# Two stacked transformer blocks on one core: norms of the second half by tile, modulation as column factors behind the transposes, the residual's affine rows inside the stages

## The reference, cut to what matters

```python
def _modulate(x, shift, scale):
    return x * (1.0 + scale) + shift

def _post_norm(x, y, gate, res_w, gain, bias):
    return _layer_norm(ALPHA * x + res_w * (1.0 + gate) * y, gain, bias)

cond = jax.nn.silu(c)                     # c: (1, 1024)
for l in range(2):
    mod = cond @ w_ada[l] + b_ada[l]      # 9 rows of 1024: shift, scale, gate of each stage
    y = _swiglu(_modulate(x, sh1, sc1), w_gate1, w_up1, w_down1)
    x = _post_norm(x, y, g1, 0.5, ln_gain[l, 0], ln_bias[l, 0])
    y = _token_mixer(_modulate(x, sh2, sc2), w_in, w_out)
    x = _post_norm(x, y, g2, 1.0, ln_gain[l, 1], ln_bias[l, 1])
    y = _swiglu(_modulate(x, sh3, sc3), w_gate2, w_up2, w_down2)
    x = _post_norm(x, y, g3, 0.5, ln_gain[l, 2], ln_bias[l, 2])
```

## Time and profile before

| | |
|---|---|
| median of 3 runs | 2457.99 us (2457.63 to 2458.3) |
| the profiled execution | 2454.0 us, its span 2452.1 us, 1.9 us around it |
| PE busy | 2270.1 us (93%), mean granted clock 0.942 |
| DVE busy | 1641.0 us (67%) |
| ACT busy | 1147.1 us (47%) |
| POOL busy | 23.9 us (1%) |
| chain that ended last | PE 86%, DVE 10%, ACT 2%, issue 1%, DMA 1% |

### The profile page before, as it was taken

One profiled execution on the slowest core, in us unless ns is written; L12 is line 12 of the kernel. 1 busy time (PEld: TensorE's weight loads), 2 busy tenths in 40 slices (PEclk: granted clock), 3 DMA queues, 4 the chain that ended last, 5 costly groups with the idle time before them and its releaser, 6 DMA issues.

```text
span 2452.1 us, 35119 instructions
## 1 busy us (share of the span) xinstructions
PE 2270.1 (93%) x13340; PEld 2022.6 (82%) x13340; DVE 1641.0 (67%) x1804; ACT 1147.1 (47%) x1433; POOL 23.9 (1%) x14
## 2 busy tenths in 40 slices
PE   7999997999999999879999998978998998968997
PEld 6889996788888899868888888967887887967886
DVE  6775766677677576657766776547776666555666
ACT  5545442545554553345544543534444554443553
POOL 0000000000000000000000000000000000000000
PEclk9998997999999999879998998979999999978999
DMA  7774320476577532108746773404763545512543
GB/s 307 287 272 142 105 102 1 189 288 246 206 290 283 184 111 103 35 25 318 282 155 253 286 272 129 172 17 182 297 249 127 199 179 188 173 52 86 199 177 120
DMA packets 59091, 446.63 MB, mean 182 GB/s; under 512 B 6912, under 2 KB 7296, under 8 KB 8320
## 3 DMA queue, kind: packets, MB, share of 16 engines
q1 hardware_dynamic: 59008, 445.45, 48.7%
HBM read 444.38 MB, written 1.05 MB: 182 GB/s over the span
## 4 chain that ended last, share of the span: by engine, by line
PE 86%; DVE 10%; ACT 2%; issue 1%; DMA 1%; POOL 0%; POOLq 0%; DVEq 0%; SPq 0%; ACTq 0%
PE ps L225 25%; PE ps L298 14%; PE ps L230 13%; PE ps L304 7%; PE ps L260 3%; PE ps L266 3%; PE ps L261 3%; PE ps L1638 2%; PE ps L280 2%; PE ps L506 2%; PE ps L207 1%; PE ps L208 1%; PE ps L213 1%; PE ps L690 1%; DVE arena L1247 1%
## 5 line engine op out<-in xcount | busy, mean ns | idle before, releaser
L192 DVE TENSOR_TENSOR w_lo<-raw,w_hi 128x1024 fp32r<-128x1024 f32 x670 | 804.9, 1222 | 395.6 <-ACT w_hi L186 395.5
L186 ACT ACTIVATE w_hi<-raw 128x1024 fp32r<-128x1024 f32 x670 | 694.4, 1052 | 496.5 <-PE ps L304 150.8
L225 PE MATMUL ps<-hT,w_hi 128*128 128x512 f32 x2752 | 687.3, 392 | 0.5 <-ACT w_hi L186 0.5
L225 PEld LDWEIGHTS ps<-hT,w_hi 128*128 128x128 f32 x2752 | 499.4, 189 | 93.3 <-ACT w_hi L186 1.0
L230 PEld LDWEIGHTS ps<-hT,w_lo 128*128 128x128 f32 x2752 | 375.4, 190 | 26.8
L230 PE MATMUL ps<-hT,w_lo 128*128 128x256 f32 x2752 | 383.7, 282 | 0.0
L298 PE MATMUL ps<-w_hi,act_hi 128*128 128x512 f32 x640 | 198.5, 391 | 0.0
L298 PE MATMUL ps<-w_hi,act_lo 128*128 128x512 f32 x640 | 197.6, 390 | 0.0
L304 PE MATMUL ps<-w_lo,act_hi 128*128 128x512 f32 x640 | 171.0, 389 | 0.0
L260 PE MATMUL ps<-w_hi,hT 128*128 128x256 f32 (+1 forms) x576 | 146.8, 290 | 2.6 <-issue 2.6
L261 PE MATMUL ps<-w_hi,hT 128*128 128x256 f32 (+1 forms) x576 | 145.1, 288 | 0.0
(11 more groups left out here) (315 smaller groups left out, 2689.4 us busy)
## 6 DMA issues: line engine op xcount, KB each, us to landing
raw<-in_g SPq DMA_DIRECT2D x88, 1024.0 KB, 4.9
raw<-in_u SPq DMA_DIRECT2D x88, 1024.0 KB, 4.9
raw<-in_d SPq DMA_DIRECT2D x88, 1024.0 KB, 6.9
arena<-in_w_ada SPq DMA_DIRECT2D x48, 1536.0 KB, 7.6
raw<-in_w_in SPq DMA_DIRECT2D x54, 1024.0 KB, 4.9
raw<-in_w_out SPq DMA_DIRECT2D x16, 1024.0 KB, 4.9
rows<-in_rows SPq DMA_DIRECT2D x13, 1024.0 KB, 9.6
arena<-in_con SPq DMA_DIRECT2D x1, 1344.0 KB, 5.5
```

Of the source, the lines that this page charges most:

```text
L186: nc.scalar.activation(w_hi[:, buf, 0:width], raw[:, slot, half * UNIT:half * UNIT + width], ACT.Copy).then_inc(unit_hi, 1)
L192: nc.vector.tensor_tensor(w_lo[:, buf, 0:width], raw[:, slot, half * UNIT:half * UNIT + width], w_hi[:, buf, 0:width].bitcast(F32), ALU.su ...
L225: nc.tensor.matmul(o, h_[:, k, c], hT[:, :, 4 * half + k, :], start=(half == k == 0), stop=False)
```

## The change

Between the stages of the second block:
- `ln_dve` goes tile by tile: gate product for tile 0 as soon as `acc_half` comes, then ALPHA * x added with the sum over columns as `accum_out`, minus the mean as a [128, 1] column; ACT squares with that column as bias and sums, then the root; DVE writes x = (tok - mean) / std. Gain and bias are not applied there.
- PE transposes `x` itself (`pre2_pe`), and `pre2_dve` applies gain * (1 + scale) and bias * (1 + scale) + shift as per-partition column factors (`gb`) when it copies the transposed blocks from PSUM to `tok`, 16 operations of 128 columns per boundary; the hi and lo split then reads `tok`.
- The residual's gain and bias rows (`affine`, two operations of 1024 columns per tile) go into the next stage: rounds 9 and 10 of an FFN, column blocks 4 to 7 of a mixer. After the last stage they follow the norm, and the output leaves in two DMAs.
- Only the gate is spread into a row, by 8 matmuls (`gate_pe`) into banks 6 and 7, copied by `gate_act` after the splits.

The modulation product is laid out transposed: `cond` is a row on all partitions, and a chunk is three multiplications of 1024 columns whose `accum_out` is one column each of `modc`, so `ada`, `cols_pe` and `cols_dve` go, in the first block too. POOL adds the bias and makes `gb` (`cols_pool`). Apart from that: `home` numbers the unit buffers through all stages, so that the next stage's unit 0 is split (`first_hi`, `first_lo`) ahead of the norm; `x` is loaded in two DMAs, `cond` later; the second block's constants are loaded in stage 6 and no longer ahead of it.

```diff
+    def first_hi(a, B, loads):
+        hi_unit(a, B, 0, 0, loads[0] + 1, 0)
+    def first_lo(v, B):
+        lo_unit(v, B, 0, 0, 0)
...
-    def pre2_dve(v, g, B):
-        shift, scale1 = mrow[:, 0, :], mrow[:, 1, :]
-        v.wait_ge(x_ready, g * 16 + 16)
-        v.wait_ge(mod_a.sem, mod_a.at("rows", g - 6))
-        nc.vector.tensor_tensor(tok[:], x[:], over(scale1, [P, TILES, D], 1), ALU.mult).then_inc(pre2_v.done("scaled"), 1)
-        v.wait_ge(pre2_v.sem, pre2_v.at("scaled", g - 6))
-        for tile in range(TILES):
-            nc.vector.tensor_tensor(tok[:, tile, :], tok[:, tile, :], shift, ALU.add).then_inc(
-                pre_v.done(f"tok{tile}"), 1)
-        pre_lo(v, g, B)
+    def pre2_pe(pe, g):
+        for name, tile, b in PIECES:
+            if b.start == 0:
+                pe.wait_ge(x_ready, g * 16 + 8 * tile + 8)
+            for k in range(4 * b.start, 4 * b.stop):
+                last = nc.tensor.transpose(tile_bank(tile)[:, k // 4, k % 4, :], x[:, tile, k * P:(k + 1) * P], IDENT)
+            last.then_inc(pre_t.done(f"trans{name}"), 1)
...
+    def pre2_dve(v, g):
+        h = g - 6
+        v.wait_ge(mod_p.sem, mod_p.at("shift", h))
+        for name, tile, b in PIECES:
+            v.wait_ge(pre_t.sem, pre_t.at(f"trans{name}", g))
+            for k in range(4 * b.start, 4 * b.stop):
+                last = nc.vector.tensor_scalar(tok[:, tile, k * P:(k + 1) * P], tile_bank(tile)[:, k // 4, k % 4, :],
+                                               gb[:, h, 0, k:k + 1], gb[:, h, 1, k:k + 1], ALU.mult, ALU.add)
+            last.then_inc(pre2_v.done(f"t{name}"), 1)
...
     def ln_act(a, h):
...
+            nc.scalar.activation(hidden[:].rearrange("p a b -> p (a b)"), tok[:, tile, :], ACT.Square,
+                                 bias=stat[:, tile:tile + 1], accum_out=stat[:, 2 + tile:3 + tile]).then_inc(
+                                     ln_a.done(f"ssq{tile}"), 1)
...
+    def ln_dve(v, h, ready):
+        v.wait_ge(gate_a, h + 1)
...
+            if tile == 0:
+                v.wait_ge(acc_half, h + 7)
+            else:
+                v.wait_ge(*ready)
...
+            nc.vector.scalar_tensor_tensor(tok[:, tile, :], x[:, tile, :], ALPHA, tok[:, tile, :], ALU.mult, ALU.add,
+                                           accum_out=stat[:, tile:tile + 1]).then_inc(ln_v.done(f"mixed{tile}"), 1)
...
+            nc.vector.tensor_scalar(x[:, tile, :], tok[:, tile, :], stat[:, tile:tile + 1], stat[:, 2 + tile:3 + tile],
+                                    ALU.add, ALU.mult).then_inc(x_ready, 8)
...
     def chunk_dve(v, n, k):
...
-            nc.vector.scalar_tensor_tensor(ada, ada_w, cond[:, bass.ds(k, 1)], ada, ALU.mult,
-                                           ALU.add).then_inc(ada_acc, 1)
...
+        for b in range(3):
+            block = ada_w[:, b * D:(b + 1) * D]
+            last = nc.vector.scalar_tensor_tensor(
+                block, block, 1.0, cond[:], ALU.mult, ALU.mult,
+                accum_out=modc[:, n, b:b + 1] if k is first_chunk else modc[:, n, bass.ds(k * 3 + b, 1)])
+        last.then_inc(ada_acc, 1)
...
+    def gate_act(a, h, half):
+        a.wait_ge(gate_t, h + 1)
```

More of the change, by code:

```diff
@@ L162, in build @@
     post_v = steps("post_v", "gained0 rstd0 gained1 rstd1")
[L163 to L167 removed]
+    pre2_v = steps("pre2_v", "t0 t1a t1b")
+    ln_v = steps("ln_v", "gated0 mixed0 neg0 gated1 mixed1 neg1 rstd0 rstd1")
+    ln_a = steps("ln_a", "table ssq0 root0 ssq1 root1")
+    gate_t, gate_a = sem("gate_t"), sem("gate_a")
+    resid = steps("resid", "gained0 added0 gained1 added1")
+    out_v = steps("out_v", "gained0 added0 gained1 added1")
+    mod_p = steps("mod_p", "biased scale gain bias shift")
     def settle(eng):
@@ new lines, in affine, with resid_dve @@
+    def affine(v, S, use, tile, which):
+        if which == 0:
+            nc.vector.tensor_tensor(x[:, tile, :], x[:, tile, :], rows[:, 0, :], ALU.mult).then_inc(S.done(f"gained{tile}"), 1)
+        else:
+            v.wait_ge(S.sem, S.at(f"gained{tile}", use))
+            nc.vector.tensor_tensor(x[:, tile, :], x[:, tile, :], rows[:, 1, :], ALU.add).then_inc(S.done(f"added{tile}"), 1)
+    def resid_dve(v, g, tile, which):
+        if tile == which == 0:
+            v.wait_ge(rows_in, g * 16 + 16)
+        affine(v, resid, g - 7, tile, which)
```

477 lines of the change are left out of this document (246 added, 231 removed).

## The result

The changed kernel runs in **2391.82 us** (median of 4 runs, 2388.78 to 2392.5) against 2458.14 (4 runs, 2457.63 to 2459.61) for the kernel before: ratio **0.9726**, 95% interval 0.9714 to 0.9738. The forecast was 2395 with a range of 2383 to 2420. The profiled execution of the changed kernel took 2392.5 us, its span is 2390.7 where it was 2452.1, and the granted clock 0.943 where it was 0.942.

A forecast was written before the change was run, and what follows sets the result against it. PE was taken as the bound, busy 93%, with its boundary waits set by a DVE chain. Gains of 61.7 + 3 + 4 + 2 less 8 for the clock make 62.7, so 2458.0 - 62.7 = 2395 us, range 2383 to 2420.

The forecast's parts named there:

- The boundary's chain: Second block's six boundaries, timed from tile 0's last matmul (T = 0): a shorter DVE chain gains 61.7 us.
- The term of the clock: Second block's six entries: PE's half clock low 4 us each in the weights, taking 8 us back, ends 0 and 16.
- The end: After the last stage: norm, affine operations and half the output end at T = 17.0 instead of 20.0, gain 3 us.
- First block and start: Column matmuls gone ahead of transposes at three boundaries, gain 4 us; ACT's first table load gone at the start, gain 2.
- Costs put at nothing: Work moved inside the stages on DVE, ACT and POOL, and the early split of unit 0: cost 0.
- Chunks: FFN rounds, 48 times: 4.4 us of DVE work for 3.4, within 3.2 us spare, cost 0; 48 us without cover.
- Affine rows inside the stages: Residual rows add 2.4 us per FFN round, in rounds without a modulation chunk, less than the chunk they replace; cost 0.
- Rival (a): DVE's accumulating form is slow and bounds six FFN stages; at half rate, 2.57 us each, the kernel takes 2463; chance 5%.
- (c): FFN rounds: DVE's slack is not one piece, chunks delay low splits PE needs, 19 us in all, 2414; chance 8%.
- (d): Second block's entries: the clock costs nothing new, 8 us less, 2387; chance 17%.
- (b): Second block's entries: the clock's low stretch reaches further, 8 us each, costing 20 instead of 8, 2407; chance 17%.
- (e): Boundaries: chain not shortened, DVE waits for ACT's roots and factor operations take their full 0.40 us, 2408; chance 3%.

The follow-up runs named there:

- both_tiles: The changed kernel with the layer norm waiting for both tiles before its first gate product: 2407.02 us, 15.2 more than the changed kernel.
- affine_at_boundary: The changed kernel with the affine rows applied at the boundary again, not inside the stages: 2416.13 us, 24.3 more than the changed kernel.
- keep_busy: The changed kernel with unread matmuls filling PE's idle time before and after the transposes at the second block's six boundaries: 2380.61 us.
- after_again: The changed kernel run and profiled once more, nothing altered: 2392.61 us.
- split_early: The changed kernel with DVE making the low splits of pieces 0 and 1a before factors and split of 1b: 2386.76 us.
- busy_early: The changed kernel with the edits of keep_busy and split_early together: 2385.38 us.
- all_gate_later: busy_early plus filler matmuls at first-block boundaries and in both blocks' mixers, with ACT's gate row copy moved behind unit 1's high part: 2359.89 us.
- chunk_plus2: The changed kernel with two more unread DVE operations of 1024 columns in each of the 48 modulation chunks: 2397.43 us.

## Why the prediction was right, step by step

The mechanism was right, and the closeness of the number is in part luck. By profiles, 62.7 us were forecast and 61.5 came. Chain and clock brought 4.3 more than forecast, the end 1.1 more, first block and start 1.6 more; against that stand 8.2 us more in the rests of stages 0 to 5, which the sum had at nothing. Either side alone would have put it 7 to 8 us off, still inside the range.

- **The boundary's chain** was right in its order and nearly in size. Predicted for the split of 1a: T = 14.0 at stage 5 to 6 and 16.0 elsewhere. Measured: 13.4, and 15.0 to 15.4. The read-out of a sum on DVE, for which I had taken ACT's 0.19 us, is 0.08; x takes 0.81 where I chose 0.75; 16 factor operations take 5.2 where 5.3 was reckoned. The boundaries still gained 70.6 us and not 61.7, and about 4 of that is one step: I let an FFN's weights start 1.2 us ahead of the split of 1a, as before, and they start 2.2 ahead. Before, PE came to them straight from its own transposes (1677.88 at stage 8), which is what set the 1.2; now they wait for ACT's high split of 1a, in the view of waits as L260 <- ACT hT L607. both_tiles and affine_at_boundary show that DVE's chain is what counts, us for us, in the two parts that they undo.
- **The term of the clock** (8 us back) was too small, and its cause was right. Low time behind the six entries is 32 us, 4.0 to 6.8 each, not 24, and the rests took 12.5 us more, not 8. keep_busy, which takes all of it away and some inside the mixers, gives 11 back. Chain and clock together brought 58.0 us where 61.7 - 8 = 53.7 was forecast. The error of the one hid half of that of the other.
- **The end** gave 4.1 for 3: the span ends 3.0 us behind the last affine row, I had allowed 3.6, and x was ready at 8.2 and not 8.5.
- **First block and start**: 6.0 at the boundaries for 4, and 1.5 for 2: the right places, and the first a third too small. **The step that failed is what I left out there**: the clock term was reckoned for the second block alone, though the change takes column matmuls away ahead of stages 1 and 4 too. The mixer of stage 4 took 1.6 us more, with 4.2 us low at its entry where before had none. That of stage 1 took 7.1 more, and none of it at the entry in this profile; low stretches inside it come and go between executions of the changed program by as much, as after_again shows (235.3), though in no profile did it reach before's 233.5.
- **Costs put at nothing.** Chunks: right, and the slack left is of one piece. That it is 2.2 us, as the sum had it (3.2 less 1.0), is luck: three multiplications with their read-outs take 3.9 us and not 4.4, so only 0.5 more than the 3.4 before, and what busy times leave is 2.7; 0.5 of that can't be used. Affine rows inside the stages: right, within 2 us. `gate_act`: right for the kernel as changed and for keep_busy. With the splits early, PE waits for the unit behind it, 0.4 us at two entries in split_early, and 1.8 at four in busy_early where the clock is up too; all_gate_later took 1.0 of each away. `first_hi` and `first_lo`, and GpSimd's new operations, were not tried by themselves.
- **Rival (a)**, the slow accumulating form, fell: 1222 ns (L1696, above), against 2570. What the Trainium skill says of this form in its Vector Engine (DVE) Microarchitecture Reference, "Points that are easy to get wrong", does not show here: both sources are float32 in SBUF, and 1024 columns with the sum take what L199, an operation of two tensors without one, takes (1226 ns). **(c)** fell with chunk_plus2. **(d)**, that the clock costs nothing new, is against the windows. **(b)** had the mechanism; the 12.5 us of the rests lie between its 20 and the forecast's 8. **(e)** fell: the factor operations end 0.32 us apart, though each is recorded at 0.40, and DVE's wait for ACT's second root is 0.65 us and inside the 8.5 that was reckoned. A slip in the working: (c)'s 2414 is 1.8% under 2458, not over 2%. TensorE: Matmul & The Clock Gate, "HAM oscillation", of the Trainium skill, which puts a return of the half clock down to waits between bursts of matmuls, agrees with this case: the weights began at 0.50 at each of the six entries, and with 8 or 20 matmuls in the idle time ahead of them they ran at 1.00.
- **Why 2391.8 and not 2395.** The forecast went from a profile 4 us under the median of its kernel, with the quickest stage 1 seen, and the changed kernel's profile lies at the top of its own runs. The medians differ by 66.3, the profiled spans by 61.5.
